# Differential attention: the combination of its two softmaxes moved from VectorE to ScalarE and GpSimd for six tiles of eight, transposes one step later, and a third buffer for the first softmax

## The reference, cut to what matters

```python
s1 = jnp.einsum('bqhd,bkhd->bhqk', a, k1).astype(jnp.float32) * scale
s2 = jnp.einsum('bqhd,bkhd->bhqk', b, k2).astype(jnp.float32) * scale
p = jax.nn.softmax(s1, axis=-1) - lam * jax.nn.softmax(s2, axis=-1)
return jnp.einsum('bhqk,bkhd->bqhd', p.astype(v.dtype), v)
```

## Time and profile before

| | |
|---|---|
| time, median of 3 runs | 3068.51 us (3068.25 to 3072.74) |
| time of the profiled execution | 3066.51 us |
| span of its profile | 3064.8 us |
| busy PE / DVE / ACT / POOL | 95% / 53% / 38% / 35% |
| differential attention | about 2517 to 2726 us of the span |

### The profile page before, as it was taken

How to read it: one execution, slowest core, us unless ns; L and a number is a source line. 1 busy time by engine, 2 the same in 40 slices (tenths; PEclk the granted TensorE clock), 3 DMA queues, 4 the chain that set the end, 5 groups by cost and what they waited for, 6 DMA issues and landing times.

```text
span 3064.8 us, 47759 instructions
## 1 busy us (share of the span) xinstructions
PE 2911.5 (95%) x17540; PEld 2508.7 (82%) x17540; DVE 1622.3 (53%) x3106; ACT 1161.2 (38%) x2101; POOL 1069.8 (35%) x690
## 2 busy tenths in 40 slices
PE   7999998999999999999999999999999987789999
PEld 6689866778888888888999988997897986678887
DVE  3899838343222232313029278982212959988861
ACT  3311264242212211213124356772322635557750
POOL 2223020432222235662225433444331544332335
PEclk9999998999999999999999999999999999999999
DMA  4123331431111113442297444313335863131223
GB/s 144 60 98 126 109 78 29 138 117 49 48 48 48 48 55 91 137 164 82 93 211 227 118 109 101 83 58 125 135 138 180 239 163 72 49 76 35 72 88 129
DMA packets 219514, 319.44 MB, mean 104 GB/s; under 512 B 81286, under 2 KB 163078, under 8 KB 217174
## 3 DMA queue, kind: packets, MB, share of 16 engines
q1 hardware_dynamic: 184774, 273.10, 30.0%
q10 hardware_dynamic: 33360, 39.98, 3.8%
q0 software_dynamic: 1216, 4.20, 0.5%
HBM read 225.76 MB, written 91.47 MB: 104 GB/s over the span
## 4 chain that ended last, share of the span: by engine, by line
PE 70%; DVE 9%; issue 3%; ACT 1%; POOL 1%; SPq 0%; DMA 0%; DVEq 0%; POOLq 0%; ACTq 0%; PEldq 0%
PE psum L2575 16%; PE psum L530 15%; PE psum L2356 8%; PE psum L2778 8%; PE psum L1085 4%; PE psum L1116 4%; PE psum L1096 3%; PE psum L794 3%; DVE arena L3195 3%; PE psum L772 2%; PE psum L783 2%; DVE diff L1475 1%; PE psum L1390 1%; PE psum L1367 1%; DVE arena L3184 1%
## 5 line engine op out<-in xcount | busy, mean ns | idle before, releaser
L2575 PE MATMUL psum<-parts_ffn 128*128 128x512 f32 x2112 | 482.0, 391 | 3.8 <-DVE parts_ffn L2532 3.8
L2575 PEld LDWEIGHTS psum<-parts_ffn 128*128 128x128 f32 x2112 | 398.2, 189 | 87.2 <-issue 2.2
L530 PE MATMUL psum<-parts_even,parts_ffn 128*128 128x256 f32 x2496 | 305.0, 285 | 3.0 <-DVE parts_ffn L2919 1.8
L530 PEld LDWEIGHTS psum<-parts_even,parts_ffn 128*128 128x128 f32 x2496 | 302.8, 193 | 3.4 <-DVE parts_ffn L2919 2.0
L2645 DVE SCALAR_TENSOR_TENSOR arena<-psum,arena 128x1023 f32<-128x1023 f32 x88 | 112.9, 1283 | 328.2 <-ACT arena L2629 322.0
L530 PE MATMUL psum<-parts_odd 128*128 128x248 f32 x2304 | 270.5, 280 | 2.7 <-DVE parts_odd L2532 1.8
L530 PEld LDWEIGHTS psum<-parts_odd 128*128 128x128 f32 x2304 | 268.3, 190 | 3.8 <-DVE parts_odd L2532 2.0
L576 ACT ACTIVATE arena<-psum 128x256 f32<-128x256 f32 (+2 forms) x240 | 87.5, 375 | 392.5 <-PE psum L530 388.7
L444 PE MATMUL psum<-parts_mixer 128*128 128x512 f32 x912 | 210.2, 391 | 0.3 <-DVE parts_mixer L287 0.3
L444 PEld LDWEIGHTS psum<-parts_mixer 128*128 128x128 f32 x912 | 170.7, 188 | 35.8 <-DVE parts_mixer L287 0.5
L2102 DVE TENSOR_SCALAR_CACHE_REDUCE choose_flags<-arena,choose_bits 128x384 uint8<-128x384 f32 (+2 forms) x198 | 174.3, 942 | 1.2
(11 more groups left out here) (370 smaller groups left out, 5889.5 us busy)
## 6 DMA issues: line engine op xcount, KB each, us to landing
arena<-ffn_up_b SPq DMA_DIRECT2D x44, 512.0 KB, 3.2
arena<-ffn_down_k SPq DMA_DIRECT2D x44, 512.0 KB, 3.7
arena<-x SPq DMA_DIRECT2D x8, 2048.0 KB, 8.7
arena<-w_in_e SPq DMA_DIRECT2D x13, 1024.0 KB, 6.7
e_tokens<-arena ACTq DMA_DIRECT2D x26, 512.0 KB, 3.1
x<-arena SPq DMA_DIRECT2D x24, 512.0 KB, 3.7
arena<-w_in_o SPq DMA_DIRECT2D x12, 992.0 KB, 6.6
o_tokens<-arena ACTq DMA_DIRECT2D x24, 496.0 KB, 3.0
```

What stands on the lines that cost most here:

```text
L530: last = pe.matmul(self.bank(t), self.hT[:, a, k, t * P:(t + 1) * P], self.weights.parts[:, self.weights.slot(s), b, k, :], start=(k, a, b ...
L2575: last = pe.matmul(self.core.psum[:, 4 * u + 2 * s + h, :], parts[:, s, a, k, :], self.hT[:, b, k, h * HALF:(h + 1) * HALF], start=(k, a, ...
```

## The change

Tiles with t in (0, 2, 3, 4, 6, 7) are combined in two instructions: ScalarE scales `p1` in place (`scale`), and GpSimd adds it to `p0` (`add`). Tiles t = 1 and 5 stay with VectorE. `p0` has a third slot, and `turn`, `high`, `low`, `attend`, `take` and `finish` of a tile come one step later. GpSimd does `add(m-1)` in its step m, behind that step's parts or `ahead` piece and behind a wait for their last semaphore. `weigh` goes ahead of `low` on VectorE. `store` moves from t = 4 to t = 7 and no longer waits for its landing.

```diff
-    HEADS, DQ, DV, LAG = 4, 64, 128, 8
-    BY_POOL = ()
+    HEADS, DQ, DV, LAG = 4, 64, 128, 9
+    BY_POOL = (0, 2, 3, 4, 6, 7)
...
-        self.p1 = own.take(2, S)
+        self.p1, third = own.take(2, S), own.take(S)
+        self.p0 = [pair[:, 0], pair[:, 1], third]
...
     def store(self, pool, i):
...
-        pool.wait_ge(self.stored[i % 2], self.stored_before[i % 2] + 16 * (i // 2 + 1))
-        pool.sem_inc(self.stage_free[i % 2], 1)
...
     def gpsimd(self, pool):
...
+        pool.wait_ge(self.v_parted, 2)
-        for m in range(self.M):
+        for m in range(self.M + 1):
             i, t = divmod(m, TT)
-            if t == 4 and i >= 1:
-                self.store(pool, i - 1)
+            if self.count(max(m - 1, 0)):
+                pool.wait_ge(self.combined[1], self.count(m - 1))
             if i + 1 < self.HEADS:
                 if t in (0, 2):
                     self.part_queries(pool, i + 1, t // 2)
+                    pool.wait_ge(self.parted[t // 2], 4 * (i + 1) + 2)
                 if t in (1, 3):
                     self.part_keys(pool, i + 1, t // 2)
+                    pool.wait_ge(self.parted[t // 2], 4 * (i + 1) + 4)
                 if t == 6:
                     self.part_values(pool, i + 1)
+                    pool.wait_ge(self.v_parted, 2 * (i + 1) + 2)
-            elif t in (4, 5, 6, 7):
+            elif t in (4, 5, 6, 7) and m < self.M:
                 self.ahead[t - 4](pool)
-            if t in self.BY_POOL:
-                self.combine(pool, m)
+                hold(pool, self.ahead_done[t - 4])
+            if m and (m - 1) % TT in self.BY_POOL:
+                self.add(pool, m - 1)
+            if t == 7 and i >= 1:
+                self.store(pool, i - 1)
         self.store(pool, self.HEADS - 1)
...
     def tensor(self, pe):
...
-            if 0 <= m - 2 < M:
-                self.turn(pe, m - 2)
+            if 0 <= m - 3 < M:
+                self.turn(pe, m - 3)
             if m < M:
                 self.scores(pe, m, 1)
-            g, h = divmod(m - 4, 2)
+            g, h = divmod(m - 5, 2)
...
+    def scale(self, act, m):
+
+        act.wait_ge(self.ratio_ready, m + 1)
+        act.activation(self.p1[:, m % 2], self.p1[:, m % 2], ACT.Copy, scale=self.ratio[:, m % 2:m % 2 + 1]).then_inc(self.weighed, 1)
+
+    def add(self, pool, m):
+
+        pool.wait_ge(self.weighed, self.count(m + 1))
+        pool.tensor_tensor(self.p0[m % 3], self.p1[:, m % 2], self.p0[m % 3], ALU.add).then_inc(self.combined[1], 1)
...
     def scalar(self, act):
...
-            if 0 <= m - 2 < M:
-                self.high(act, m - 2)
+            if 0 <= m - 3 < M:
+                self.high(act, m - 3)
             if m < M:
                 self.exps(act, m, 0)
-            if m % 2 == 0 and 0 <= m - 6 < M:
-                self.take(act, (m - 6) // 2)
+            if 0 <= m - 1 < M and (m - 1) % TT in self.BY_POOL:
+                self.scale(act, m - 1)
+            if m % 2 and 0 <= m - 7 < M:
+                self.take(act, (m - 7) // 2)
             if m < M:
                 self.exps(act, m, 1)
...
     def vector(self, dve):
...
             if m < M:
                 self.peak(dve, m, 0)
+            if 0 <= m - 1 < M:
+                self.weigh(dve, m - 1)
             for h in range(2):
-                if 0 <= m - 2 < M:
-                    self.low(dve, m - 2, h)
+                if 0 <= m - 3 < M:
+                    self.low(dve, m - 3, h)
             if m < M:
                 self.peak(dve, m, 1)
-            if 0 <= m - 1 < M:
-                self.weigh(dve, m - 1)
-                if (m - 1) % TT not in self.BY_POOL:
-                    self.combine(dve, m - 1)
-            if m % 2 and 0 <= m - 7 < M:
-                self.finish(dve, (m - 7) // 2)
+            if 0 <= m - 1 < M and (m - 1) % TT not in self.BY_POOL:
+                self.combine(dve, m - 1)
+            if m % 2 == 0 and 0 <= m - 8 < M:
+                self.finish(dve, (m - 8) // 2)
```

More of the change, by code:

```diff
@@ L1251, in __init__ @@
         self.loads_after, self.first_free, self.rest_free = loads_after, first_free, rest_free
-        self.pe_after, self.act_after, self.ahead = pe_after, act_after, []
+        self.pe_after, self.act_after, self.ahead, self.ahead_done = pe_after, act_after, [], []
         self.M = self.HEADS * TT
-        self.pT, self.p0 = shared
+        self.pT, pair = shared
         there = [shaped(a, (3, S)) for a in sets[0:2]], sets[2].rearrange("p (a t d) -> p a t d", a=2, d=P)
@@ L1267, in __init__ @@
             s(f"{name}_{x}") for x in ("scored", "peaked", "neg_ready", "shifted", "expd"))
-        self.inverted, self.ratio_ready, self.combined = s(f"{name}_inverted"), s(f"{name}_ratio_ready"), core.sems(f"{name}_combined", 2)
+        self.inverted, self.ratio_ready, self.weighed = s(f"{name}_inverted"), s(f"{name}_ratio_ready"), s(f"{name}_weighed")
+        self.combined = core.sems(f"{name}_combined", 2)
         self.turned, self.high_out, self.low_out = s(f"{name}_turned"), s(f"{name}_high_out"), s(f"{name}_low_out")
@@ L1274, in __init__ @@
             core.pool_stored_count[c] += 16 * self.HEADS // 2
-        self.stage_free = core.sems(f"{name}_stage_free", 2)
-        self.done = [(self.stage_free[c], self.HEADS // 2) for c in range(2)]
+        self.done = [(self.stored[c], core.pool_stored_count[c]) for c in range(2)]
         self.exps_done = [(self.expd, 2 * self.M)]
@@ L1329, in store, with count @@
         pool.dma_start(dst, self.os_[:, i % 2]).then_inc(self.stored[i % 2], 16)
-        pool.wait_ge(self.stored[i % 2], self.stored_before[i % 2] + 16 * (i // 2 + 1))
-        pool.sem_inc(self.stage_free[i % 2], 1)
+    def count(self, m):
+        return [n % TT in self.BY_POOL for n in range(m)].count(True)
     def gpsimd(self, pool):
@@ L1376, in turn @@
                 b = 4 * h + j
-                last = pe.transpose(self.core.psum[:, 4 + h, j * P:(j + 1) * P], self.p0[:, m % 2, b * P:(b + 1) * P], self.core.ident)
+                last = pe.transpose(self.core.psum[:, 4 + h, j * P:(j + 1) * P], self.p0[m % 3][:, b * P:(b + 1) * P], self.core.ident)
             last.then_inc(self.turned, 1)
@@ L1423, in exps @@
             act.wait_ge(self.shifted, m + 1)
-            if m >= 2:
-                act.wait_ge(self.turned, 2 * (m - 2) + 2)
-            dst, bias = self.p0[:, m % 2], self.bias[:, m % 2:m % 2 + 1]
+            if m >= 3:
+                act.wait_ge(self.turned, 2 * (m - 3) + 2)
+            dst, bias = self.p0[m % 3], self.bias[:, m % 2:m % 2 + 1]
         else:
@@ L1488, in weigh, with combine @@
                           ALU.mult, ALU.mult).then_inc(self.ratio_ready, 1)
[L1490 to L1494, removed]
+    def combine(self, dve, m):
+        dve.wait_ge(self.ratio_ready, m + 1)
+        dve.scalar_tensor_tensor(out=self.p0[m % 3], in0=self.p1[:, m % 2], scalar=self.ratio[:, m % 2:m % 2 + 1],
+                                 in1=self.p0[m % 3], op0=ALU.mult, op1=ALU.add).then_inc(self.combined[0], 1)
     def low(self, dve, m, h):
@@ L1503, in finish @@
         if t == 0 and i >= 2:
-            dve.wait_ge(self.stage_free[i % 2], i // 2)
+            dve.wait_ge(self.stored[i % 2], self.stored_before[i % 2] + 16 * (i // 2))
         dve.wait_ge(self.backed, g + 1)
@@ L4036, in build @@
         place = (start + 7) // 8 * 8
-        own = Region(core, "diff", place, 18 * S + 416)
+        own = Region(core, "diff", place, 19 * S + 416)
         there = [core.placed(f"diff_even{n}", core.parts_at + at, words, F32R) for n, (at, words) in enumerate(((16 * S, 3 * S), (10 * S, 3 * S), (13 * S, 2 * S)))]
@@ L4044, in build @@
         diff_rows, diff_gate, latent_rows = (block4(place + 4 * S * n) for n in range(3))
-        combine_at = place + 18 * S + 416
+        combine_at = place + 19 * S + 416
         gate_at = core.words - 4 * S
@@ L4068, in build @@
                       latent_scores(1), lambda pool: latent.part_values(pool, 0, 1)]
+        diff.ahead_done = [[(latent.parted[s], count)] for s in range(2) for count in (5, 7)]
         core.open_parts("parts_odd_out")
```

## The result

The changed kernel takes 3088.42 us, median of 7 runs (3083.26 to 3095.20), beside 3072.74 for the kernel before in its own 7 (3068.25 to 3077.57). The ratio is 1.0052, 95% interval 1.0041 to 1.0064. So the change costs 0.5%, some 16 us. The forecast said slower by 8.7 us, and 3077 with a range up to 3087: the direction was right, the size was not, and the time lies 1.4 us above the range. (The kernel before took 4.2 us more in these runs than in the three that the forecast started from; 3068.51 by the ratio would be 3084.5.)

The account below looks back on a forecast made before the run. The prediction took the chain through take to bound odd steps and VectorE's order the others. A stage ending 6.7 us late plus 2 for the clock made 8.7 us over the median 3068.5: 3077 us, range 3063 to 3087.

Parts of the forecast that it names:

- The steps with take: Odd steps, where attend waits for ScalarE's take: the added scaling lengthens each from 5.83 to 6.89 us.
- VectorE's relief: Combinations taken off VectorE: worth nothing net up to tile 28, as they lie beside the chain through take.
- this chain: Exponential, scaling, take, attend, scores, peak, next exponential in odd steps: 5.83 + 1.06 = 6.89 us.
- The clock inside the stage: TensorE's granted clock between tiles 7 and 28: taken to stay at 1.00, so no cost was added there.
- The even steps: Steps without take: 4.83 us each by VectorE's order, 5.75 where VectorE keeps the combination.
- The third rival: Lock adds 12 us less the 2 counted, longer gaps lower TensorE's clock inside the stage: some 3088 us; chance 0.16.
- The lock: VectorE's remaining combinations and GpSimd block each other: 2 us over steps 7 to 28.
- Up to tile 7: From exps(0,1) to exps(7,1), before any take: 35.6 us, a gain of 4.0.
- The end: From exps(28,1) to the latent stage: add(27) queues behind GpSimd's latent pieces; 6.7 us late, plus 2 for the clock.
- GpSimd's row: GpSimd's unbroken work from the end of add(26), landing included, to add(31): 36.3 us.
- VectorE was the bound: Rival: two steps cost 9.8 or 8.9 us, 98.4 plus some 5 for steps 7 to 27; 3050 us; chance 0.14.
- the middle's: Steps 7 to 27, from exps(7,1) to exps(28,1): 130.7 us, a loss of 3.3.

Follow-up runs that it names:

- e4: The changed kernel plus 12 TensorE matmuls that nobody reads, ahead of attend's wait for take; ratio to the kernel before 1.0034, median 3077.41 us.
- e1: The changed kernel with take ahead of the scaling in ScalarE's odd steps; ratio to the kernel before 1.0006, median 3070.76 us.
- e5: The changed kernel with take moved ahead of exps(m,0) in the odd steps; ratio to the kernel before 0.9965, median 3067.38 us.
- e11: e9 with all combinations back on VectorE (BY_POOL empty); ratio to the kernel before 0.9981, median 3062.82 us.
- e9: e6 with GpSimd's first latent piece a step later, behind add(28); ratio to the kernel before 0.9921, median 3042.05 us.
- e2: The changed kernel with all combinations on VectorE (BY_POOL empty), its other edits kept; ratio to the kernel before 1.0006, median 3069.00 us.
- e10: The changed kernel with the edits of e1 and e4 together; ratio to the kernel before 0.9991, median 3066.51 us.
- e3: The changed kernel with GpSimd's add ahead of pieces in the last head, latent loads let go at step 24; ratio to the kernel before 1.0042, median 3080.49 us.
- e6: The changed kernel with the edits of e5 and e3 together; ratio to the kernel before 0.9915, median 3050.10 us.

## Why the prediction was right and where it failed

**The steps with take: right.** The step that the forecast put at 6.89 us took 6.85 wherever the clock was granted in full, in the changed kernel (two steps) and in e4 (ten). e1 and e5, which move nothing but `take`, changed the time by 0.5% and 0.9%. That VectorE's relief lies beside this chain is shown from both sides. Where `take` is out of the way, the relief wins 16 us between tiles 7 and 28 (e11 to e9). Where it isn't, it wins 1.6 with the scaling behind `take` (129.0 in e2, 127.4 in e1), and with the scaling ahead of it 9.7 are lost (138.7).

**The clock inside the stage: the step that failed.** The forecast's sum gave it 0 and put the 2 us for the clock at the end only. It argued from a quiet stretch of the kernel before, with gaps of 1.25 us. But its own chain said that attend would wait 1.06 us longer, and the gap came to 2.2 us, or to 3.06 and more behind a step in which VectorE still combines. Behind nine of the eleven gaps the granted clock fell, and each time the step took 8.4 us for 6.85: nine times 1.55 us are 14 us, which e4 and e10 show to be the clock's. Why it spared the steps 13 and 25, with gaps of 2.27 and 2.23, stays open. The kernel before had shown such a fall inside the stage already, in its step 15, where a combination in the lock kept TensorE waiting for 3.42 us:

```profile
2616.00:2622.00 6.00, 2.58 (x12) 0.81 1.04 340
...
2619.50 1.78 PE L1377 MATMUL psum<-arena,both 128*128 128x128 f32 x8 [3.42 <-DVE both L1493]
2620.93 2.06 PE L1367 MATMUL psum<-diff_even 128*128 128x512 f32 x4
```

The four scores matmuls took 2.06 us there, not 1.09 to 1.17. The forecast read only the quiet steps.

The even steps took some of the 14 us back: they had 4.25 to 4.65 us and 5.19 to 5.51 where the forecast had 4.83 and 5.75, together 3.4 us less, and the 2 us for the lock did not come here. The net is the 8.0 us between 130.7 and 138.7.

The third rival named the clock with a chance of 0.16. Its 3088 is what came, but by luck in part: its other half, a lock that costs 12 us, did not come, and no sum of its own gave the clock's share.

**The lock: a small term, and set too high for its place.** The eight combinations left on VectorE take 13.6 us in total, where 8 x 1.28 = 10.2 would be free of it. But 2.4 of the 3.4 us over lie in the steps 2 and 6 and 0.7 in step 30. For the steps 7 to 28 the sum had 2 us, and 0.2 came. The head's parts met the combinations less often there than laid out; in e5, with shorter steps, they met three times more.

**Up to tile 7: right.** 35.9 us, 35.6 forecast.

**The end: right mechanism, terms too small.** add(27) stood behind the pieces, exps(29,1) stood for 8.2 us, e3 took 8.8 us of it away. Of 39.2 + 2 forecast, 43.2 came. GpSimd's row took 39.5 us and not 36.3, and from its end to the latent stage it was 9.8 and not 7.8; the row began 6.1 us ahead of exps(28,1) and not 4.9. Landing was 9.3 us and not 7.0: the same loads took longer from SyncE's issue (2697.41) to the first cast (2706.44), 9.0 beside 6.8. In e1, e4, e5 and e10, whose GpSimd has the same order, this took 6.3 to 7.6, so the change does not cause the 9.0; no run here tells what does. I left out store(2), which the change moves to t = 7: 0.9 us between add(30) and add(31), where it is in the row. Behind the row turn(31) started 2.1 us after add(31) had ended, since an attend group at the lower clock (2.88 us for 1.65) stood ahead of it.

**The sum.** The forecast's terms against before were -4.0 up to tile 7, +3.3 to tile 28, and +7.4 and +2 at the end, 8.7 us. Measured: -3.7, +11.3 and +11.4, 19.0 us. Of the 10.3 us between, 8.0 are the middle's.

**"VectorE was the bound": false for this change, and yet the reason why e9 pays.** The 3050 that this rival gave is close to e6's 3050.10 by chance, since that is on a chip where the kernel before took 3076.43. Its 98.4 us and 5 for GpSimd between tiles 7 and 28 are nearer: 106.5 to 107.1 came in e5, e6 and e9.

## What to carry to other kernels

When work is taken off a busy engine, look at the order of the engine that gets it: here a scaling of 1.15 us was put ahead of a 0.37 us copy on which TensorE was waiting. That one place cost 11.3 us between tiles 7 and 28. With the copy ahead of the exponential too, the same work was 32 us faster there, and only then was VectorE's relief worth its 16 us. A wait that the profile gives no releaser for is worth matching by hand, to the tenth of a microsecond, against ends on other engines, before the busy shares are believed. Work done ahead of its time hurts nobody on an engine with nothing else to do. It becomes a wall when something on the critical path is queued behind it, and with a load in it the wall includes the landing. And where a change makes TensorE's gaps longer than those of the quiet steps, look for gaps of that length elsewhere in the trace of before, and give the clock a term of its own in the sum.

## What the runs showed of the hardware that was not expected

TensorE's granted clock fell behind single gaps of 2.0 to 4.0 us inside a stage in which it was busy 76 to 79% of the time (the two windows of the changed kernel), and the fall cost 1.5 us in each step. It did not fall behind every such gap: 2.23 and 2.27 us in the changed kernel, 2.04 in e2 and 2.40 in the kernel before left it at 1.00, while 2.03 in another step of e2 did not. The gaps of 1.18 to 1.26 us ahead of attend in the kernel before and in e1 never had a fall behind them. What else decides stays open. Matmuls whose result nobody reads, put into the gap, kept it at 1.00 and made the stretch between tiles 7 and 28 faster, by 10.6 us in e4 and by 10.5 in e10. The Trainium skill, TensorE: Matmul & The Clock Gate, section HAM oscillation — how this bites in real kernels, tells of a kernel that waits for loads between short bursts of matmuls and starts each burst at the lower clock; this trace agrees, with 8.4 us for 6.9 in nine steps of eleven, though here the wait is for another engine.
